# A two-layer hybrid decoder trunk on one core: the delta rule's and linear attention's outputs turned on VectorE, weight transfers begun earlier outside the mixers, and x's last low halves ahead of its sums

## What is computed

```python
def hybrid_layer(x, norm_g, w_in, w_out, ...):
    h = rms_norm(x, norm_g)
    p = jnp.einsum('btd,dp->btp', h, w_in)
    (aq, ak, av, alr, az, bq, bk, bv, bz, cq, ck, cv, cz, dqkv, dbeta, da, dz) = jnp.split(p, offs, axis=-1)
    ya = gla_mixer(aq, ak, av, alr, gla_w_lr2, gla_b_lr2, gla_norm_g) * jax.nn.silu(az)
    yb = swa_mixer(bq, bk, bv, swa_q_norm_g, swa_k_norm_g, swa_sinks, slopes_b) * jax.nn.silu(bz)
    yc = diff_mixer(cq, ck, cv, ...) * jax.nn.silu(cz)
    yd = gdn_mixer(dqkv, dbeta, da, gdn_conv_w, gdn_A_log, gdn_dt_bias, gdn_norm_g) * jax.nn.silu(dz)
    y = jnp.concatenate([ya, yb, yc, yd], axis=-1)
    return x + jnp.einsum('btm,md->btd', y, w_out)
```

## Time and profile before

| | us |
|---|---|
| median of three runs | 1816.85 |
| the runs | 1816.59, 1816.85, 1820.76 |
| the profiled execution | 1817.91 |
| its span | 1816.1 |
| PE busy in it | 1806.1 (99%) |
| PEld, POOL, DVE, ACT busy | 1484.4, 920.1, 854.8, 505.0 |

### The profile page before, as it was taken

One profiled execution on the slowest core, in us unless ns is written; L12 is line 12 of the kernel. 1 busy time (PEld: TensorE's weight loads), 2 busy tenths in 40 slices (PEclk: granted clock), 3 DMA queues, 4 the chain that ended last, 5 costly groups with the idle time before them and its releaser, 6 DMA issues. The chain is left out here.

```text
span 1816.1 us, 23463 instructions
## 1 busy us (share of the span) xinstructions
PE 1806.1 (99%) x9382; PEld 1484.4 (82%) x9382; DVE 854.8 (47%) x1829; ACT 505.0 (28%) x967; POOL 920.1 (51%) x864
## 2 busy tenths in 40 slices
PE   9999999999999999999999999999999999999999
PEld 7788888888888888788877888888888878877887
DVE  7546815523333443544534478264333344445342
ACT  6213114022222543322312131141222235433220
POOL 5555544545555444445465555445455454444454
PEclk9999999999999999999999999999999999999999
DMA  7566545645555547456765665555555565474556
GB/s 273 169 186 208 175 152 160 186 143 183 177 175 181 163 140 243 129 161 185 233 213 181 191 203 176 158 155 171 162 178 177 169 184 156 148 242 134 160 170 209
DMA packets 94508, 324.99 MB, mean 179 GB/s; under 512 B 10144, under 2 KB 10688, under 8 KB 94144
## 3 DMA queue, kind: packets, MB, share of 16 engines
q1 hardware_dynamic: 43904, 155.73, 27.8%
q0 software_dynamic: 40320, 146.82, 26.7%
q10 hardware_dynamic: 10176, 20.94, 3.2%
HBM read 315.05 MB, written 8.40 MB: 178 GB/s over the span
## 5 line engine op out<-in xcount | busy, mean ns | idle before, releaser
L509 POOL TENSOR_TENSOR w_lo<-w_raw,w_hi 128x512 fp32r<-128x512 f32 x575 | 759.5, 1321 | 650.3 <-DMA w_hi<-in_wstream 488.4
L552 PE MATMUL acc<-w_hi,actT_hi 128*128 128x512 f32 x1408 | 559.8, 398 | 0.0
L552 PE MATMUL acc<-w_hi,actT_lo 128*128 128x512 f32 x1408 | 548.9, 390 | 0.0
L552 PE MATMUL acc<-w_lo,actT_hi 128*128 128x512 f32 x1408 | 548.5, 390 | 0.0
L552 PE MATMUL acc<-actT_hi,w_hi 128*128 128x512 f32 x896 | 358.4, 400 | 4.3 <-POOL w_lo L509 2.6
L552 PE MATMUL acc<-actT_hi,w_lo 128*128 128x512 f32 x896 | 349.6, 390 | 0.0
L552 PE MATMUL acc<-actT_lo,w_hi 128*128 128x512 f32 x896 | 349.2, 390 | 0.0
L552 PEld LDWEIGHTS acc<-w_hi,actT_lo 128*128 128x128 f32 x1408 | 264.3, 188 | 55.9
L552 PEld LDWEIGHTS acc<-w_hi,actT_hi 128*128 128x128 f32 x1408 | 264.5, 188 | 55.1 <-issue 2.8
L552 PEld LDWEIGHTS acc<-w_lo,actT_hi 128*128 128x128 f32 x1408 | 264.7, 188 | 51.7
L484 POOL DMA_DIRECT2D w_hi<-in_wstream x280 | 159.8, 571 | 234.6 <-PE acc L552 230.3
(11 more groups left out here) (264 smaller groups left out, 1586.2 us busy)
## 6 DMA issues: line engine op xcount, KB each, us to landing
w_raw<-in_wstream SPq DMA_DIRECT2D x288, 512.0 KB, 4.5
w_hi<-in_wstream POOLq DMA_DIRECT2D x280, 512.0 KB, 3.8
out_x<-slots ACTq DMA_DIRECT2D x7, 1024.0 KB, 7.1
slots<-in_x ACTq DMA_DIRECT2D x1, 4096.0 KB, 19.5
slots<-out_x ACTq DMA_DIRECT2D x1, 4096.0 KB, 19.2
slots<-in_x SPq DMA_DIRECT2D x3, 1024.0 KB, 12.0
slots<-rows ACTq DMA_DIRECT2D x2, 1024.0 KB, 5.7
out_x<-slots ACTq DMA_DIRECT2D x4, 256.0 KB, 2.1
```

Of the source, the lines that this page charges most:

```text
L509: pool.tensor_tensor(w_lo[:, n % RING], w_raw[:, g % RAW, k], w_hi[:, g % HI, k].bitcast(F32), ALU.subtract).then_inc(w_ready, 1)
L552: last = nc.tensor.matmul(acc[b][:, :], lhsT, rhs, start=(k == 0 and i == 0), stop=(k == kts - 1 and i == 2))
```

## The change

1. **dz and az are turned on DVE.** `turn_blocks` turns 32 x 32 squares: for each 32 partitions of source and target one transpose of 4 x 4 x 32 columns, 16 for each of dz and az. They go from slot 3 to slot 10 and from slot 5 to slot 13, eight of dz's in linear attention's tile 0 and eight in tile 1 (four ahead of the wait for the scores, four after the gate), four of az's in each of the window's tiles. PE's `turn_y` is left for blocks 8 to 15; 8 to 11 stand together ahead of o0's kt 2. `y_hi` and `y_lo` read slots instead of PSUM for blocks 0 to 7. cq and cz change slots (to 3 and 5), and so do buffers of `dif`. ACT's read of x for the residual now stands behind `y_hi` 0 to 7 and `take_out` of cz.
2. **High halves ahead of both low halves** in the pairs `dense_only` (a layer's first 8 and last 8 pairs): POOL issues the next pair's `w_hi` ahead of the present pair's waits. Elsewhere the order stays.
3. **x's last low halves first.** Low halves 12 to 15 stand ahead of the sums over blocks 8 to 11. Lambda's small sums move behind the first convolution; the taps are halved at the start.

```diff
+Y_TURNED = dict(dz=10, az=13)
...
+                    follows = FIRST_HI <= g + 1 < DEPTH * PAIRS
+                    dense_only = i < KT // 2 or i >= PAIRS - LAST_KTS // 2
+                    if follows and dense_only:
+                        high_halves(g + 1)
                     pool.wait_ge(raw_in[g % RAW], g // RAW * 16 + 16)
...
-                        if k == 0 and FIRST_HI <= g + 1 < DEPTH * PAIRS:
+                        if k == 0 and follows and not dense_only:
                             high_halves(g + 1)
...
-                    def y_first(k, l=l):
-                        if k == KT - 1:
-                            for m in range(4):
-                                turn_y(l, m)
...
                             pe.wait_ge(S_DVE.sem, S_DVE.at(l, f"ylo{k}"))
-                            for m in (4 + 2 * k, 5 + 2 * k):
-                                if m < 3 * HEADS:
+                            if k == 2:
+                                for m in range(2 * HEADS, 3 * HEADS):
                                     turn_y(l, m)
...
+                def turn_blocks(c, rows):
+
+                    src = slot(SLOT[c]).rearrange("p t (h c) -> p t h c", h=HEADS)
+                    dst = slot(Y_TURNED[c]).rearrange("p h (t c) -> p t h c", t=TILES)
+                    for r in rows:
+                        rs_ = slice(BLK * r, BLK * r + BLK)
+                        for f in range(P // BLK):
+                            fs = slice(BLK * f, BLK * f + BLK)
+                            dve.transpose(dst[fs, :, :, rs_], src[rs_, :, :, fs]) \
+                                .then_inc(Y_DVE.sem, Y_DVE.one(f"{c}{r}{f}"))
...
+                    if t < 2:
+                        turn_blocks("dz", [2 * t])
                     w(A_PE, "a")
...
                     gate(A_DVE, l, t, gz, V["GATE"])
+                    if t < 2:
+                        turn_blocks("dz", [2 * t + 1])
...
                     gate(B_DVE, l, t, gz, W["GATE"])
+                    turn_blocks("az", [t])
...
+                    if t == TILES - 1:
+                        for k in range(HEADS):
+                            y_lo(k)
                     w(B_PE, "pv")
...
-                x_group(l, 3)
-                if l == 0:
-                    lambdas()
+                x_low_halves(l, 3)
+                x_total(l, 2)
+                x_pairs(l, 3)
+                x_total(l, 3)
```

More of the change, by code:

```diff
@@ L1308, in _, with y_hi @@
                     nc.scalar.activation(sa, sa, ACT.Exp, scale=-0.5).then_inc(*s("ro"))
+                    if CHUNKS[8 + t] == "cq":
+                        act.wait_ge(Y_DVE.sem, Y_DVE.at(l, f"dz{P//BLK-1}{P//BLK-1}"))
                     take_out(l, CHUNKS[8 + t])
+                def y_hi(k):
+                    if k < 12:
+                        act.wait_ge(kt_done, kt_value(l, IN_KTS - KT + k))
+                    if k < 2 * HEADS:
+                        c = ("dz", "az")[k // HEADS]
+                        act.wait_ge(Y_DVE.sem, Y_DVE.at(l, f"{c}{P//BLK-1}{P//BLK-1}"))
+                        src = slot(Y_TURNED[c])[:, k % HEADS]
+                    else:
+                        act.wait_ge(S_PE.sem, S_PE.at(l, f"yT{k}"))
+                        src = mix[k % 4][:, :]
+                    nc.scalar.activation(actT_hi[:, k], src, ACT.Copy, scale=pcv(l, PC["y"] + k)) \
+                        .then_inc(S_ACT.sem, S_ACT.one(f"yhi{k}"))
                 def squares(t):
@@ L1377, in _ @@
                         take_out(l, "cv")
-                def y_hi(k):
-                    if k < 12:
-                        act.wait_ge(kt_done, kt_value(l, IN_KTS - KT + k))
-                    act.wait_ge(S_PE.sem, S_PE.at(l, f"yT{k}"))
-                    nc.scalar.activation(actT_hi[:, k], mix[k % 4][:, :], ACT.Copy,
-                                         scale=pcv(l, PC["y"] + k)) \
-                        .then_inc(S_ACT.sem, S_ACT.one(f"yhi{k}"))
+                for k in range(2 * HEADS):
+                    y_hi(k)
+                take_out(l, "cz")
                 act.wait_ge(B_DVE.sem, B_DVE.at(l, f"{TILES-1}.y3"))
@@ L1391, in _ @@
                 act.dma_start(xT, (out if l else x).rearrange("(k p) n -> p k n", p=P)).then_inc(xres_in, 16)
-                for k in range(4):
+                for k in range(2 * HEADS, 3 * HEADS):
                     y_hi(k)
-                take_out(l, "cz")
-                for k in range(4, 12):
-                    y_hi(k)
+                act.wait_ge(S_DVE.sem, S_DVE.at(l, f"ylo{2*HEADS-1}"))
                 def dif_scale(t):
@@ L1537, in gate, with x_group @@
                 dve.scalar_tensor_tensor(Zs, tmp, 1.0, Zs, ALU.add, ALU.mult).then_inc(St.sem, St.one(f"{t}.g3"))
+            def x_group(l, n):
+                x_low_halves(l, n)
+                x_pairs(l, n)
+                x_total(l, n)
             dve.wait_ge(norm_in, 16)
-            for n in range(3):
+            taps = pcol_all[:, :, PC["conv"]:]
+            dve.tensor_scalar(taps, taps, 0.5, None, ALU.mult).then_inc(taps_halved, 1)
+            for n in range(2):
                 x_group(0, n)
-            lambda_sums()
+            x_low_halves(0, 2)
+            x_pairs(0, 2)
             for l in range(DEPTH):
@@ L1937, in add @@
                         dve.tensor_tensor(xs, acc[b][:, :], xs, ALU.add).then_inc(acc_free, 1)
-                for k in range(12):
+                for k in range(HEADS, 3 * HEADS):
                     y_lo(k)
```

76 lines of the change are left out of this document (46 added, 30 removed).

## The result

The changed kernel takes 1807.76 us (median of 5, 1806.13 to 1811.08), the kernel before 1816.59 us beside it (median of 5, 1815.61 to 1820.76): ratio 0.9942, 95% interval 0.9929 to 0.9955, so 0.6% faster. The forecast was 1805.8 us in a range of 1803.8 to 1810.5. The profiled execution is the slowest of the five, 1811.08 us with a span of 1809.3.

The account below looks back on a forecast made before the run. PE, busy 99% of the span, was taken to bound the kernel. Gains of 7.0 + 4.0 + 0.1 = 11.1 us took 1817.9 to 1806.8 profiled, 1805.8 us against the median; range 1803.8 to 1810.5.

Parts of the forecast that it names:

- Transposes off PE: PE in cz and o0: 32 transposes a layer leave, 3.48 us a layer, 7.0 us in all.
- rival E: A transpose on PE is worth its recorded 272 ns: 17.4 us gained instead of 7.0, so 1795.4; chance 0.01.
- DVE's transposes: DVE's new 512-column transposes: 0.73 us each from start to start, bounds 0.44 and 1.32.
- Rival B: DVE's transposes cost for each 32 x 32 square: slower, 1825 us at 2.1 us a transpose; chance 0.03.
- The state's slack: Linear attention's tiles 0 and 1: state ready 0.3 to 1.2 us before PE uses it; cost 0, range 0 to 2.
- rival A: Linear attention's state comes late for PE: 4.8 to 8.4 us in all at 1.32 us a transpose, 1810.6 to 1814.2; chance 0.11.
- Behind the gate, window, y: DVE's transposes behind linear attention's gate and in window tiles, and the `y_lo` and `y_hi` work: cost 0.
- The border: Between layers: PE's three stalls for `w_lo` all go with high halves issued earlier, 4.0 us gained.
- Rival C: The border stays: full DMA engines make landings late, the border still loses up to 4 us, 1809.8; chance 0.08.
- Part 3: x's low halves: 0.1 us of gain, bounds -0.3 and +0.8.
- The moved 4 MB read: Read now starting near o0 delays the pair for o0's kts 6 and 7; slack some 3 us, cost 0, up to 2 a layer.
- rival D: The residual read hurts o0: 1 to 2 us a layer, 1807.8 to 1809.8; chance 0.07.

Follow-up runs that it names:

- e1: Changed kernel with the early high halves and x's new order undone, the turning on DVE kept: 1810.45 us.
- e2: Kernel before with only the next pair's high halves ahead of both low halves, in a layer's first and last pairs: 1814.83 us.
- e4: Changed kernel with DVE doing the four transposes ahead of the masked scores twice, in linear attention's tiles 0 and 1: 1821.5 us.
- e5: Changed kernel with all eight transposes of linear attention's tiles 0 and 1 behind the gate, none ahead of the masked scores: 1807.54 us.
- e8: Changed kernel with the next pair's high halves ahead of both low halves in all pairs, inside the mixers too: 1825.43 us.
- the second profile: Changed kernel itself, unchanged, run and profiled once more: 1807.42 us, span 1805.2.
- e9: Changed kernel with all eight transposes behind the gate, row-sum broadcast ahead of ACT's dv gate, x group 1's totals behind the last residual add: 1806.61 us.

## Why the prediction was right

- *Transposes off PE, 7.0 us.* Right: 2 x (2.59 + 1.04) = 7.26, alone in e1, absent in e2. cz lost 2.59 (2.6 forecast), o0 1.04 (0.9); o1 is 0.06 longer. Starts, not records, were the price: rival E, 17.4 us by 272 ns each, falls. The remaining sixteen are recorded with 1.91 us, as in the earlier trace rows.
- *DVE's transposes, 0.73 us.* Right: four in a row take 2.90 us, recorded 703 ns each. Rival B has no ground, and no cost of the added dimension can be seen.
- *The state's slack, 0.3 to 1.2 us, cost 0.* Half right. The slack was 0.85 to 1.08 us in 23 of 28 tiles, inside the forecast; e4 agrees (state 3.2 us later, 2.1 waited). Two things were taken too favourably. DVE's end of its transposes was read once, at 424.49, and the 1.14 us of idle behind it spent as free; in five tiles the end came 1.1 us later. And the step from the masks to the state's end was bounded by 3.72 us, where it took 478.42 to 482.50, 4.1 us, in tile 1; the trace of before already had 3.88 in tile 2 of layer 0. So rival A's effect came true by two collisions with `w_lo` together, not by a slow transpose, in five of 28 tiles, at 1.4 us each: some 1 us an execution that the sum had at 0.
- *Behind the gate, window, y: 0.* Right; e5 shows that eight fit behind the gate.
- *The border, 4.0 us.* Right: 4.06 in eight profiles with part 2, 3.39 and 3.76 in the changed kernel's two, 3.82 in e8. A pair's first `w_lo` was ready there 1.7 to 3.1 us ahead of use in the changed kernel's two, for 3.6 forecast. "What is late next there is nothing I can see" was wrong by a little: DVE's sums behind the pairs of `w_lo`. It looked only at who waits for `w_lo`, not at whom `w_lo` holds up. Rival C falls: no landing at the border took over 7.3 us with part 2, of 9.6 that were allowed.
- *Part 3, 0.1 us.* Not resolved; noise of 2 us at the start is larger.
- *The moved 4 MB read, 0.* Right. The pair's `w_hi` was issued at 703.10 (704 forecast) and its `w_lo` began at 712.06 (714.2 forecast); PE has no wait in all of o0, and rival D falls:

```profile
712.06 1.29 POOL L519 TENSOR_TENSOR w_lo<-w_raw,w_hi 128x512 fp32r<-128x512 f32 x1 [7.08 <-DMA w_hi<-in_wstream]
```

- *The sum.* 11.1 us forecast; the second profile has 10.9 less span, the first 6.8. The forecast median was 1805.8 and the measured ones are 1807.76 and 1807.42: inside the range, the first just above the 1804.5 to 1807.5 that had a chance of 0.70. Of the 1.6 to 2.0 us between, about 1 us is in terms that the sum did not have, the state's collisions and the delta rule's wait, since e9, which has neither, takes 1806.61. The other 0.8 us stays open; the kernel before itself had medians from 1816.59 to 1818.98 in its sets of five and more. The delta rule's wait stood in no rival. DVE's wait for the rows was there before (2.19 us), and how far it may slip before PE waits (3.5 us) could have been asked for.
- *A slip of reading.* The waits of the earlier trace rows are 6.8 us in all, not less than 6; nothing in the sum rests on it.
